# Expert weights asked for one stage earlier, and six experts in fixed places

## The reference, cut to what matters

```python
scores = sigmoid(x2 @ w_router)                       # 64 experts
_, idx = top_k(scores + router_bias, 6)
gate = take(scores, idx); gate = gate / sum(gate) * 2.5
for each expert e, its tokens xb:
    hb = silu(xb @ w_gate[e]) * (xb @ w_up[e])        # 1024 -> 256
    acc[tokens] += (hb @ w_down[e]) * gate            # 256 -> 1024
x = layer_norm(alpha * x + acc + shared_expert(x2))
```

## Time and profile before

| | |
|---|---|
| median of 3 runs | 2112.52 us (2109.18 to 2113.34) |
| profiled execution, its own time | 2109.84 us |
| its span in the profile | 2108.1 us |
| TensorE matmul busy | 1896.3 us, 90% of the span |
| VectorE busy | 798.8 us, 38% |
| DMA | 541.68 MB, mean 257 GB/s |
| sigmoids of expert passes (L671) | 72, from 436.0 to 2041.3 us |
| SP issues of expert matrices in the loop of layer 0 | from 419.96 us |

### The profile page before, as it was taken

The page is one execution under the profiler, slowest core; times in us unless marked ns, Lnnn a source line. Parts: engine busy times, 40 slices in busy tenths (PEclk is TensorE's granted clock), DMA queues, the critical chain, the costliest instruction groups (busy, mean ns, idle before and its releaser), DMA issues. The chain is left out here.

```text
span 2108.1 us, 33033 instructions
## 1 busy us (share of the span) xinstructions
PE 1896.3 (90%) x11136; PEld 1140.6 (54%) x11137; DVE 798.8 (38%) x2140; ACT 374.5 (18%) x840; POOL 297.4 (14%) x385
## 2 busy tenths in 40 slices
PE   9999999878999989888999779999878999997877
PEld 4475544445666545444444448874445666664443
DVE  3100653622333322226267654434622333332226
ACT  2000650100111111120244422210101111111010
POOL 7000000011111111110015413110011111111110
PEclk9999899989999999999999769999989999999999
DMA  6210201699999999996222110022699999999987
GB/s 240 80 61 0 91 26 51 277 409 393 412 421 421 420 421 420 421 380 245 70 61 79 35 34 1 2 81 76 277 374 408 394 423 422 422 423 424 424 373 287
DMA packets 143873, 541.68 MB, mean 257 GB/s; under 512 B 30878, under 2 KB 68310, under 8 KB 93998
## 3 DMA queue, kind: packets, MB, share of 16 engines
q1 hardware_dynamic: 122478, 490.19, 58.0%
q0 software_dynamic: 21312, 50.37, 6.1%
HBM read 521.58 MB, written 46.14 MB: 269 GB/s over the span
## 5 line engine op out<-in xcount | busy, mean ns | idle before, releaser
L664 PE MATMUL bank<-W,XT 128*64 128x256 f32 x2880 | 333.0, 388 | 72.6 <-issue 37.0
L664 PEld LDWEIGHTS bank<-W,XT 128*64 128x64 f32 x2880 | 236.8, 140 | 180.6 <-issue 61.2
L699 PE MATMUL bank<-W,ht 128*64 128x512 f32 x720 | 167.8, 608 | 12.9 <-DMA W<-in_w_exp_down_dram 8.3
L1923 PE MATMUL bank<-XT,rwkv_room 128*128 128x512 f32 x352 | 157.2, 601 | 0.0
L1206 PE MATMUL bank<-XT,foxw 128*128 128x512 f32 x320 | 137.8, 592 | 0.0
L675 DVE TENSOR_TENSOR sig<-sig,bank 128x256 f32<-128x256 f32 x72 | 30.3, 422 | 282.1 <-ACT sig L671 251.5
L1923 PEld LDWEIGHTS bank<-XT,rwkv_room 128*128 128x128 f32 x352 | 66.6, 192 | 84.2 <-issue 83.8
L677 DVE TENSOR_TENSOR h<-sig,bank 128x256 f32<-128x256 f32 x72 | 30.4, 422 | 209.1 <-PE bank L664 209.0
L664 PE MATMUL bank<-third_high,XT 128*64 128x256 f32 x864 | 99.0, 380 | 7.2 <-DMA third_high<-in_w_exp_up_dram 7.2
L699 PE MATMUL bank<-third_high,ht 128*64 128x512 f32 x432 | 98.7, 597 | 7.0 <-DMA third_high<-in_w_exp_down_dram 3.9
L699 PEld LDWEIGHTS bank<-W,ht 128*64 128x64 f32 x720 | 55.2, 138 | 89.6 <-issue 79.9
(11 more groups left out here) (425 smaller groups left out, 2818.8 us busy)
## 6 DMA issues: line engine op xcount, KB each, us to landing
W<-in_w_exp_gate_dram SPq DMA_DIRECT2D x88, 1024.0 KB
W<-in_w_exp_up_dram SPq DMA_DIRECT2D x88, 1024.0 KB
W<-in_w_exp_down_dram SPq DMA_DIRECT2D x88, 1024.0 KB
third_high<-in_w_exp_up_dram SPq DMA_DIRECT2D x40, 1024.0 KB
third_high<-in_w_exp_down_dram SPq DMA_DIRECT2D x40, 1024.0 KB
rwkv_room<-in_w_exp_gate_dram SPq DMA_DIRECT2D x20, 1024.0 KB
third_low<-in_w_exp_gate_dram SPq DMA_DIRECT2D x20, 1024.0 KB
W<-y_rows SPq DMA_DIRECT2D x8, 2048.0 KB, 20.6
```

What stands on the lines that cost most here:

```text
L664: last = pe.matmul((gate, up)[m][64 * a:64 * a + 64, :], xt[s][:, k, 64 * a:64 * a + 64], weights(w, a, m)[:, k * FE:(k + 1) * FE], start= ...
L699: last = pe.matmul(B[5 + half][64 * a:64 * a + 64, :], ht[:, j, 64 * a:64 * a + 64], weights(w, a, 2)[:, at:at + 512], start=(j == 0), sto ...
L1923: last = pe.matmul(main(i)[:], wc[i % WBUFS][:, kb, :], K.XT[:, kb, :], start=(kb == 0), stop=(kb == KD - 1))
```

## The change: what it does

- In the output projection SP asks for ten of the twelve matrices of pairs 0 and 1. In layer 1, where five of the ten places still hold `w_out`, those five are asked for after the last product of the projection, and the stores of x rows are behind them on SP's queue. The norm's vectors and the router move to the places of the other two matrices (`LAST_PLACES`), which are asked for in the tables.
- In the tables SP asks for those two and for the two gate matrices of pair 2. Up and down of pair 2 stay at the start of the loop.
- For that pair 2 is made of experts 4 and 5, whatever their load: `FIXED` is 6, 58 experts are sorted, and the deal skips pair 2's place.
- Place 2's gate matrices lie in a `room` of 16 KB per partition that now exists for the whole program. Input weights, attention buffers and RWKV chunk tiles are carved out of it in other stages, so that SBUF holds it all. The one-hot table `hot` becomes bfloat16.

```diff
-FIXED = 4
-SORTED_PAIRS = PAIRS - FIXED // 2
+FIXED = 2 * WSLOTS
 ROUNDS = 5
-HALF = SORTED_PAIRS // ROUNDS // 2
+HALF = (PAIRS - 2) // ROUNDS // 2
...
-    ranked = K.rank_at[:, FIXED:E].rearrange("p (i j k) -> p i j k", i=ROUNDS, k=2)
+    ranked = K.rank_at[:, 4:E].rearrange("p (i j k) -> p i j k", i=ROUNDS, k=2)
...
-                (K.e_col16[:], [[0, 1]], 0, 1), (K.is_sorted[:], [[0, 1]], 0, 1), (K.rank_at[:, 0:FIXED], [[1, FIXED]], 2 * E, 0),
-                *((ranked[:, :, HALF * h:HALF * h + HALF, :], [[2, ROUNDS], [2 * ROUNDS, HALF], [1, 2]], 2 * ROUNDS * HALF * (1 - h), 0)
-                  for h in range(2))):
+                (K.e_col16[:], [[0, 1]], 0, 1), (K.is_sorted[:], [[0, 1]], 0, 1),
+                *((ranked[:, :, HALF * h:HALF * h + HALF, :], [[2, ROUNDS], [2 * ROUNDS, HALF], [1, 2]], 2 * (ROUNDS * HALF - 1) * (1 - h), 0)
+                  for h in range(2)),
+                (K.rank_at[:, 0:FIXED], [[1, FIXED]], 2 * E, 0)):
...
-        hot = sb("hot", [P, NT * TOPK, E])
+        hot = sb("hot", [P, NT * TOPK, E], BF16)
...
-                for i in range(2):
-                    for m in range(3):
-                        for a in range(2):
-                            load_expert(K, sp, L, 2 * i + a, i, a, m)
+                for slot, a, m in LAST_PLACES:
+                    load_expert(K, sp, L, 2 * slot + a, slot, a, m)
+                for a in range(2):
+                    load_expert(K, sp, L, 4 + a, 2, a, 0, [[K.room[:, 0, :], K.room[:, 1, :]]])
                 sp.wait_ge(K.x_stored, 16 * NT * (L + 1))
...
-                first_third = experts_of(2)
-                for m in range(3):
+                for m in range(1, 3):
                     for a in range(2):
-                        load_expert(K, sp, L, first_third[a], 2, a, m, third)
+                        load_expert(K, sp, L, 4 + a, 2, a, m, third)
...
+LAST_PLACES = ((1, 1, 1), (1, 1, 2))
...
 class OutWeights:
+    places = ()
...
 class LateOutWeights:
+    places = ((0, 1, 0), (0, 1, 1), (0, 1, 2), (1, 0, 1), (1, 0, 2))
...
     (output_projection)
+        places = [(slot, a, m) for slot in range(2) for m in range(3) for a in range(2) if (slot, a, m) not in LAST_PLACES]
+        later = [place for place in places if place in w_out.places]
+        free = [place for place in places if place not in later]
...
                 shared.load(sp)
+                for slot, a, m in free:
+                    load_expert(K, sp, L, 2 * slot + a, slot, a, m)
+                if later:
+                    sp.wait_ge(made, 2 * (NT - tiles_ready))
+                for slot, a, m in later:
+                    load_expert(K, sp, L, 2 * slot + a, slot, a, m)
                 for t in range(NT):
                     sp.wait_ge(ln.done, 2 * t + 2)
                     sp.dma_start(K.x_rows[t * P:(t + 1) * P, :], X[:, t, :]).then_inc(K.x_stored, 16)
```

More of the change, by code:

```diff
@@ L554, in expert_loop @@
         ht = sb("ht", [P, 2, P])
-        low = next_weights.room if next_weights is not None else sb("third_low", [P, 2, KD * FE])
         high = sb("third_high", [P, 4, KD * FE])
-        third = [[low[:, 0, :], low[:, 1, :]], [high[:, 0, :], high[:, 1, :]], [high[:, 2, :], high[:, 3, :]]]
+        third = [[K.room[:, 0, :], K.room[:, 1, :]], [high[:, 0, :], high[:, 1, :]], [high[:, 2, :], high[:, 3, :]]]
         ending = Combination(K, L, scope, shared, out, next_weights, high)
@@ L1124, in fox_layer @@
         NB = 4
-        wc = [sb(f"foxw{s}", [P, KD, WC]) for s in range(NB)]
+        wc = [K.room[:, s, :].rearrange("p (k n) -> p k n", k=KD) if s < 2 else sb(f"foxw{s}", [P, KD, WC])[:] for s in range(NB)]
         wf = sb("foxwf", [P, KD, NH])
@@ L1382, in attention @@
         blocks = max(NT if kind == "tok" else NMEM // P for kind, i in pairs)
-        prob = [sb(f"prob{s}", [P, blocks * P]) for s in range(BUFS)]
-        probT = [d["probT"] if s == 0 and "probT" in d else sb(f"probT{s}", [P, 2, blocks, T])[:] for s in range(2)]
+        taken = 2 * blocks * T
+        probT = [d["probT"], K.room_flat[:, 0:taken].rearrange("p (e b t) -> p e b t", e=2, b=blocks)]
+        if taken + BUFS * blocks * P <= 2 * KD * FE:
+            prob = [K.room_flat[:, taken + s * blocks * P:taken + (s + 1) * blocks * P] for s in range(BUFS)]
+        else:
+            prob = [sb(f"prob{s}", [P, blocks * P])[:] for s in range(BUFS)]
         nmax = sb("nmax", [P, BUFS])
@@ L1733, in sb @@
                 return scope.enter_context(nc.sbuf_tensor(f"rwkv_{name}", shape, dt))
-            room = sb("room", [P, 2, KD * FE])
-            weights = RwkvWeights(K, scope, R, j, room)
+            weights = RwkvWeights(K, scope, R, j)
             finish_last(weights)
@@ L1757, with __init__ @@
 class RwkvWeights:
-    def __init__(self, K, scope, R, j, room):
-        flat, at = room[:].rearrange("p a n -> p (a n)"), [0]
+    def __init__(self, K, scope, R, j):
+        flat, at = K.room_flat, [0]
         def carve(parts, n):
@@ L1765, in carve @@
             return flat[0:parts, at[0] - n:at[0]]
-        self.I, self.R, self.j, self.room = K.in_, R, j, room
+        self.I, self.R, self.j = K.in_, R, j
         self.src = K.in_["rwkv_w_in"][j].rearrange("(p k) n -> p k n", k=KD)
@@ L2260, in rwkv_chunks, with carve @@
         attend(first_chunk)
-        Z, U = sb("Z", [P, NH, HD]), sb("U", [P, NH, HD])
+        room = [0]
+        def carve(shape):
+            n = int(np.prod(shape))
+            room[0] += n
+            return K.room_flat[:, room[0] - n:room[0]].rearrange("p (a b) -> p a b", a=shape[0])
+        Z, U, diag = carve((NH, HD)), carve((NH, HD)), carve((NH, P))
+        yT = carve((1, TILES * P))[:, 0, :]
         g2, g2_loaded = sb("g2", [P, TOKW]), sem("g2_loaded")
         S = [sb(f"S{s}", [P, TILES, HD]) for s in range(2)]
-        yT, dev, sq = sb("yT", [P, TILES * P]), sb("dev", [P, TILES * P]), sb("sq", [P, TILES * P])
-        diag = sb("diag", [P, NH, P])
+        dev, sq = sb("dev", [P, TILES * P]), sb("sq", [P, TILES * P])
         center = sb("center", [P, P])
@@ L2556, in _ @@
                     act.wait_ge(z_made, n)
[L2557 removed]
+                    act.activation(by_parity(Z, 0), state_bank(0), ACT.Copy).then_inc(z_even, 1)
                     if c:
@@ L2636, in _ @@
                     dve.wait_ge(z_made, n)
-                    dve.tensor_copy(by_parity(Z[:], 1), state_bank(1)).then_inc(z_odd, 1)
+                    dve.tensor_copy(by_parity(Z, 1), state_bank(1)).then_inc(z_odd, 1)
                     if n < NT:
@@ L2640, in _ @@
                     dve.wait_ge(u_made, n)
-                    dve.tensor_copy(by_parity(U[:], 1), state_bank(1)).then_inc(u_odd, 1)
+                    dve.tensor_copy(by_parity(U, 1), state_bank(1)).then_inc(u_odd, 1)
                     if c:
@@ L2681, in shared_state @@
     K.arena = K.W[:].rearrange("p a b c d -> p (a b c d)")
+    K.room = sb("room", [P, 2, KD * FE])
+    K.room_flat = K.room[:].rearrange("p a n -> p (a n)")
     K.k_kept = nc.dram_tensor("k_kept", [HD, NMH, NMEM], F32).ap()
```

11 lines of the change are left out of this document (5 added, 6 removed).

## The result

The changed kernel takes 2120.10 us (median of 8 runs, 2117.09 to 2122.01); the kernel before, run beside it, 2110.99 us. The ratio is 1.0046, 95% interval 1.0036 to 1.0056: 9.7 us slower by the ratio, 9.1 us between the two medians. The forecast was 2119.0 us, slower. The profiled execution of after took 2122.01 us (span 2120.3), 12.2 more than before's profiled one; so its trace shows somewhat more of a loss than the medians do.

What follows compares the result with a forecast made beforehand. The DMA stream, 16.9 us a pair against TensorE's 14.4, was taken to bound the expert loops. Layer 0's 0 and layer 1's +6.6 us gave 2112.52 + 6.5 = 2119.0 us, range 2109 to 2126.

Steps and rivals of the forecast that it cites:

- The end is pair 5's refill plus a fixed load: Expert loops: each layer ends at pair 5's refill (527.2 and 1639.5) plus a fixed load of 24 pairs.
- Output projection and tables cost 0: Stages before the expert loops: early weight loads fit in idle DMA; cost 0 in the projection, gain 0 in the tables.
- The preload turns into a hole: Loop start: 5.0 us of loads removed leaves DMA empty from about 430 to 436.2; 0 in layer 0.
- rival 1: Loop start: pass 0's 8.4 us stand vanishes and the preload pays, together -8 us, 2104.5; chance 0.16.
- The stand of pass 0 is code behind data: Loop start: TensorE's 8.40 us stand is its code fetched behind DMA data and stays; taken as 0 (-1 to +1).
- each first visit has a stand: Expert loops: TensorE's stands of 8.40, 8.48 and 2.77 us are all first visits to a branch of the pass.
- The extra pass: Layer 1: pair 2 needs two passes, putting one extra pass ahead of pair 5's refill; +6.6 us (0 to +12.8).
- pass 2: Layer 1's loop: sigmoid at 1575.9 (bounds 1573.7 and 1577.9), against 1577.9 before.
- pass 3: Layer 1's loop: pair 2 again, 12.8 us plus 2 for code from idle DMA (bounds 0 and 10.1), to 1590.7.
- pass 4: Layer 1's loop: pair 3, first visit of another branch, stall taken as 4 us (bounds 0 and 10.1), to 1607.5.
- Two of my own signs of being wrong: Changed profile: TensorE's stands moved or vanished; expert loads slowed the output projection.
- rival 3: Layer 1: the extra pass counts in full because a long stall falls on pass 4 or 3; +12 to +14, 2125; chance 0.12.

Runs made afterwards that it cites:

- the hold in the kernel before: Kernel before, SP asking for pair 2's six matrices only after TensorE's very first expert product of the loop: 2113.33 us, ratio 1.0021.
- the preload alone: Changed kernel with the six fixed experts undone (four fixed, pair 2's six matrices asked for at the loop's start, other early loads kept): 2110.03 us, ratio 0.9997.
- the hold: Changed kernel, SP asking for pair 2's up and down only after TensorE's first expert product of the loop: 2116.89 us, ratio 1.0031 to the kernel before.
- the short queue: Kernel before with pass 0 without branches and pair 5's six matrices asked for only after the fourth pass's gate product: 2122.97 us, ratio 1.0056.
- the straight kernel: Kernel before with the three branches left out of pass 0 alone, which always uses place 0: 2104.72 us, ratio 0.9989.
- the fixed experts alone: Kernel before with six fixed experts in place of four, all loads where they were: 2122.19 us, ratio 1.0050.
- the changed kernel with pass 0 straight: Changed kernel with the branches left out of pass 0: 2115.31 us, ratio 1.0033 to the kernel before.

## Why the prediction was right, and where only its total was

- **The end is pair 5's refill plus a fixed load: right for this change.** From that refill to the last sigmoid layer 1 took 401.8 us before (1639.50 to 2041.3) and 401.2 after (1652.35 to 2053.5). It needs the stream to be dry at the refill. With the hold in the kernel before it was not dry, and from a refill 4.7 us earlier layer 0 ended 0.7 us later.
- **Output projection and tables cost 0: right**, shown by the preload alone (0.9997). In layer 1's projection after is 5.6 us behind by its end, but with TensorE's clock at 0.50, which also happens without the loads (below).
- **The preload turns into a hole: right.** Empty from 431 to 438 as forecast; layer 0 later by 1.0, inside the 0 +/- 1. My rival 1, that the preload pays because the stand of pass 0 vanishes, is refuted by the stand itself (8.05 us). Layer 1's hole ahead of its second refill is there too, at 4.5 us (the windows from 1584 to 1596) for the 5 to 8 that I gave.
- **The stand of pass 0 is code behind data: half right.** Taking the data away leaves 4.9 of 8.05 us, taking the branch away leaves none. It is code by the packet of the instruction queue (427.16 in before), but the data only slow it: in the fourth pass's stands such packets came 5.6 to 6.2 us apart at a DMA share of 1.00 to 1.03 (two steps, of 5.0 and 3.4 us just before the stream ran dry, apart), with the hold and the short queue 3.0 to 3.5 us apart at 0.03 to 0.72, and the three of the straight kernel's longer stand came at the same pace as the two of the shorter. A fetch behind all the data would not do that; the rival given for the short queue, a fetch that takes its turn with the data, fits better. And the reading that each first visit has a stand is too wide: layer 0's second and third passes are first visits and have none in before.
- **The extra pass: right in place and sign, its size too low.** The forecast moved pair 5's refill by 6.6 us; it moved by 12.85. Term by term: pass 2 came at 1578.0, for 1575.9 (+2.1, at my upper bound); pass 3 took 14.5 us for 14.8; pass 4 took 21.2 for 16.8 (+4.4); the next three passes 38.4 for 38.4. The mis-sized term is pass 4's. I gave 4 us to the first visit of another branch, since only one pair's gate and up lay ahead of its code. That short queue didn't make the wait short, with DMA full (0.96 and more from 1596 to 1608): it cost 5.28 us of stand, with one packet of code, at 1601.80, and 2.9 more, as the products after it ran at a clock of 0.50 up to 1613.0 (10.04 us for 64 products, 7.1 in an ordinary pass). The two passes were over an ordinary one by 1.7 + 8.4 us, where before's fourth pass was over by 10.1. That the sums are equal may be chance: with the fixed experts alone it is 0.0 + 8.1, in the changed kernel with pass 0 straight 6.5 + 7.4. In each the two together were over by more than the 6 us that I had let them cost.
- **Two of my own signs of being wrong came up.** A stand of TensorE moved (layer 1's, from the fourth pass to the fifth), and that is where the size went wrong. Layer 1's output projection was longer; that didn't decide the time, as the preload alone shows.
- **So the mechanism of rival 3 (the pass counts in full) is what the trace shows in layer 1.** The total still came near the forecast, 2120.1 for 2119.0, in part by luck: I added 6.5 us, where the medians differ by 9.1, to a median of three runs (2112.52) that was 1.5 us above that of the eight runs beside the changed kernel (2110.99). The ratio gives 9.7 us (7.6 to 11.8) where the two profiled executions differ by 12.2. The fixed experts alone give 10.5 us (7.6 to 13.3), which does not reject 12.8. The profiled execution of before was 1.2 us under the median of the runs beside it, and that of after 1.9 over; I did not find where that difference lies.

## What to carry to other kernels

Before moving a load ahead, find what the next load behind it waits for: if that event does not move, the freed bandwidth becomes a hole, as it did here with 2.1 MB a layer. A rule that fixes the order of work regardless of its size is to be priced at the place where the big item now falls; here one item of 69 tokens over a limit of 64 cost as much as a whole pass, because it came ahead of the refill that sets the end. And taking away one jump can lengthen the stand at the next (here from 8.87 to 14.64 us, with three packets of code in it for two): count the packets in each stand before counting the gain.

## What the runs showed of the hardware

- In TensorE's long stands at first jumps into code one to three packets of 16 KB begin on the instruction queue (q8). At a DMA share of 1.00 to 1.03 those within one stand of the fourth pass were 5.6 to 6.2 us apart in 24 steps (before: 472.75 and 478.44; the straight kernel: 464.44, 470.29, 476.31). Two steps shortly before the engines ran dry were shorter at a share that was still full: 5.0 us at 0.99 (the changed kernel with pass 0 straight: 477.28 and 482.26) and 3.4 at 1.00 (the short queue: 469.94 and 473.34). At lower shares it was 3.45 us at 0.42 (the hold: 423.31 and 426.76), 3.26 at 0.39 (the short queue: 473.34 and 476.60), then 3.24 at 0.72 and 2.99 at 0.03 (the short queue in layer 1: 1590.72, 1593.96, 1596.95). How many weights were queued made no difference in the first step, 5.85 us in the straight kernel and 5.86 with the short queue; what made the two steps at a full share short is not shown.
- The stand at pass 0 (one packet) was 4.8 to 5.3 us where the loads were held and 7.4 to 8.4 us with them; at the fourth pass the stands with two packets took 8.5 to 9.2 us and those with three 11.5 to 14.8 us, but for one of 4.9 us with two packets (the changed kernel with pass 0 straight, layer 1, 1581.09 to 1585.99, DMA at 0.41 between the two); in layer 1 with its extra pass the stand at the fifth pass was 4.7 to 5.9 us. Not every first visit has a stand: layer 0's second pass has none in before. From 491 to 930 in layer 0 no such packet comes, and the longest time that gate or up products stand there is 2.08 us in before (758.63 to 760.71), ended by a load of weights.
- The packets above stand at the jumps. Without the branch at pass 0 its products follow without a stand in all four kernels that have it so (421.19 to 422.02 in layer 0, where the others begin them at 425.7 to 429.8).
- A long stand was paid twice. At layer 1's fifth pass in after the granted clock fell to 0.50 at 1606.2, in the stand, and stayed there until 1613.0, so that the 64 products behind it took 10.04 us, 7.1 in an ordinary pass. In before it was 0.50 from 475.9 to 486.1, from inside the fourth pass's stand until 4.6 us behind it. At pass 0 little of this is the stand's own: without a stand its 64 products took 8.81 us, with one 8.50 to 9.97 in layer 0.
- In layer 1 the granted clock fell to 0.50 for 17 us, between 1479 and 1503.4, from the last part of the output projection into the tables, in six of the twelve profiled executions, with the expert loads there (after, the preload alone, the hold) and without them (fixed experts alone, the hold in the kernel before, the short queue). In the other six, again of both kinds, it was 1.00 in the output projection and fell to 0.50 for 3.4 to 6.8 us in the tables, between 1498 and 1515. In after the output projection ended 5.6 us later than in before (1495.36 for 1489.74), 0.9 of which it had at the first of its last 64 products (1448.99 for 1448.06), and TensorE's first transposes of the loop came 2.8 us later, as before had its own dip in between.
